# A two-layer decoder step in three-product fp32r: the product with the weight's lower half moves to the end of each unit, three bits of work move on VectorE

## Chip, core, metric

One NeuronCore of a Trainium2 chip runs the whole program. TensorE (PE; PEld is its weight load), VectorE (DVE), ScalarE (ACT), GpSimd (POOL) and SyncE (SP) run side by side and meet at semaphores. The metric is device microseconds of one execution; lower is better.

## The reference

Two layers over 288 tokens (256 of a prompt, 32 of eight samples), width 1024:

```
h = RMSNorm(x); z = h @ w_in                 # u, v, B, C, xin, gate_A, gate_B
ya = (gelu(u) * spatial_mix(RMSNorm(gelu(v)))) @ w_a
yb = (B * conv3(C * xin)) @ w_b
x += (sigmoid(gate_A) * ya + sigmoid(gate_B) * yb) @ w_o
x += PEER(RMSNorm(x))                        # 16384 experts, 8 heads, top 16 of 128 x 128 keys
x += sigmoid(RMSNorm(x) @ w_pg) * (p @ w_ple)
y = RMSNorm(x) after layer 2
```

The output also holds the convolution's last rows and the samples' normalised v.

## The kernel before

**Units.** All weights stream through SBUF in tiles of 128 x 1024, four tiles to a quad, 91 quads to a layer. A tile is a *unit*: ACT rounds the raw tile to `w_hi` (fp32r, semaphore `hi`), DVE or POOL makes the rest `w_lo = raw - w_hi` (semaphore `lo`), and PE adds up in one PSUM bank, over eight chunks c of 128 rows, three products: w_hi with the activation's upper half (line 1417), w_hi with its lower half (line 1418), w_lo with the upper half (line 1419). That is 24 matmuls. Before its first matmul a unit waits for `lo` (and for `evac`, that its bank is empty). `raw` has four slots and `w_hi`, `w_lo` two each, so ACT rounds unit j+2 once PE is done with unit j (`mm`), and DVE makes its `w_lo` behind that (`ahead`, line 865).

**Stages of a layer.** Quads 0 to 13 are w_in, 14 to 23 w_a, w_b, w_o, w_q, all with 288 columns. Then come 32 quads of the experts' u table with 256 columns: 16 in *fine segments* (POOL makes `w_lo` in halves, line 388; `lo_half` and `lo` tell PE; `mm_half` tells ACT that the first four chunks are done), 16 in *mixing quads*, where PE puts groups of small fp16 one-hot matmuls (lines 1597, 1598) between the units. Then 32 quads of the v table (lines 1621 to 1623), w_ple with PE transposes between its units, and w_pg (the gate).

**Seams.** Where one stage's output is the next one's input, the activation must be split too: ACT rounds chunk c (`upper`, semaphore `op_hi`), DVE makes the lower half (`lower` or `lower_scaled`, lines 898, 904, 1012; semaphore `op_lo`). The next stage's first unit (`first_quad`) waits for `op_lo` chunk by chunk. In the loops that end a stage, DVE does for each chunk: empty the PSUM bank, `ahead`, then `lower`.

**Squares.** Before a norm ACT squares x (`sq`, the tile `ext`), POOL adds up the eight chunks (`sum_chunks`, line 312), and PE sums over partitions with a matrix of ones (`sum_squares`, lines 1402 and 1406) behind unit 1 of the next quad (unit 2 at a layer's start). For the gate POOL adds chunks 0 to 5 and PE takes the last two itself (`direct=2`). The root (ACT) and its reciprocal (DVE, line 887) follow.

Each engine works its queue in the order of the code; there is no planner.

Of the kernel before, what the change touches and what calls it, by code (L numbers as in the profile page):

```python
# [4 lines left out]
P = 128  # L5
DEPTH = 2
D = 1024
C = D // P
# [68 lines left out]
def hybrid_trunk(nc, stream, u_rows, x_in, pe_in, conv_in, gains_in, ws_in, ws_blk_in, bias_in, keys_in,  # L77
                 y_out, conv_out, v_out):
    ctx = ExitStack()
    with ctx:  # L80
# [217 lines left out]
        def _(pool):  # L298
# [20 lines left out]
            for L in range(DEPTH):  # L319
# [113 lines left out]
                sum_chunks(L * SQUARES + 3 * C, direct=2)  # L433
# [7 lines left out]
        def _(act):  # L441
# [19 lines left out]
            for L in range(DEPTH):  # L461
# [84 lines left out]
                with act.Fori(0, 2) as i:  # L546
                    for j in range(4):
                        step(i + 2, j)
                        gelu(i * 4 + (8 + j))
                        act.wait_ge(t_ok, L * T_OPS + i * 4 + (j + 1))  # L550
                        upper(unit_ap(b_hi, i * 4 + j), unit_ap(t_op, i * 4 + j))
                        act.activation(unit_ap(sq, i * 4 + j), unit_ap(z, i * 4 + j), ACT.Square).then_inc(sq_ok, 1)
# [276 lines left out]
        def _(dve):  # L829
# [29 lines left out]
            for L in range(DEPTH):  # L859
# [71 lines left out]
                with dve.Fori(0, 2) as i:  # L931
                    for j in range(4):
                        evacuate(i + 2, j, unit_ap(z, i * 4 + (8 + j)), root[:, :])
                        normalised(0, i * 4 + j, x)
                        ahead(i + 2, j)
                        lower(i * 4 + (C + j), i * 4 + j, b_hi, b_lo, t_op)
# [70 lines left out]
                with dve.Fori(0, 2) as i:  # L1007
                    for j in range(4):
                        evacuate(i + Q_A, j, unit_ap(z, i * 4 + (40 + j)), unit_ap(z, i * 4 + (40 + j)))
                        ahead(i + Q_A, j)  # L1010
                        dve.wait_ge(op_hi, L * PREPS + i * 4 + (3 * C + j + 1))
                        dve.tensor_tensor(unit_ap(b_lo, i * 4 + j), unit_ap(z, i * 4 + (32 + j)),
                                          unit_ap(b_hi, i * 4 + j).bitcast(F32), ALU.subtract).then_inc(op_lo, 1)
# [3 lines left out]
                with dve.Fori(0, 2) as i:  # L1017
                    for j in range(4):
                        evacuate(i + Q_B, j, unit_ap(t_op, i * 4 + j), unit_ap(z, i * 4 + (48 + j)))
                        dve.wait_ge(evac, L * EVACS + i * 4 + (4 * Q_B + j + 5))  # L1020
                        dve.tensor_tensor(unit_ap(t_op, i * 4 + j), unit_ap(t_op, i * 4 + j),
                                          unit_ap(z, i * 4 + (40 + j)), ALU.add).then_inc(t_ok, 1)
                        ahead(i + Q_B, j)
                        lower(i * 4 + (4 * C + j), i * 4 + j, h_hi, h_lo, t_op)
# [307 lines left out]

# [62 lines left out]
        def _(pe):  # L1395
# [13 lines left out]
            for L in range(DEPTH):  # L1409
# [3 lines left out]
                def product(out, j, col, rhs_hi, rhs_lo, first, last):  # L1413

                    wh = w_hi[:, j % 2, col:col + P]
                    wl = w_lo[:, j % 2, col:col + P]
                    pe.matmul(out, wh, rhs_hi, start=first, stop=False)  # L1417
                    pe.matmul(out, wh, rhs_lo, start=False, stop=False)  # L1418
                    return pe.matmul(out, wl, rhs_hi, start=False, stop=last)  # L1419

                def unit(q, j, evac_q, a_hi, a_lo):

                    pe.wait_ge(lo, u0 + q * 4 + (j + 1))
                    pe.wait_ge(evac, e0 + evac_q * 4 + (j + 1))
                    for c in range(C):
                        m = product(ps[:, j, 0:T], j, c * P, a_hi[:, c, :], a_lo[:, c, :], c == 0, c == C - 1)
                    m.then_inc(mm, 1)
# [10 lines left out]

                def first_quad(q, n, skipped=0, a_hi=h_hi, a_lo=h_lo, squares=None,
                               order=range(C), until=(0, 0, 0, 0), squares_at=1, direct=0, after=0):  # L1440

                    for j in range(after, 4):
# [7 lines left out]
                        for k, c in enumerate(order):  # L1450
                            if j == 0:
                                operand(n + k + 1)
# [315 lines left out]
```

## Time and profile before

| | |
|---|---|
| time, median of 3 runs (lowest, highest) | 2280.68 us (2279.29, 2281.01) |
| span of the profiled execution | 2278.8 us |
| PE busy | 2246.9 us (99%), 15796 matmuls |
| PEld, DVE, ACT, POOL busy | 92%, 75%, 60%, 38% |
| HBM | 203 GB/s over the span |

The profiled execution was not timed by itself. Its span, from first to last instruction, is 0.5 us under the fastest run and 1.9 us under the median. Matmuls are pipelined: one of 256 columns is shown as 0.28 us long but the next starts 0.12 us later. So a wait on PE is read from the distance of two starts; "idle" in the trace counts less of it.

### The profile page before, as it was taken

To read this page: it belongs to the slowest core of one execution; us is meant where nothing else is said; L and a number is where in the kernel's file an instruction comes from. 1 tells how busy PE (TensorE), PEld (TensorE's weight loads), DVE (VectorE), ACT (ScalarE), POOL (GpSimd) and SP (SyncE) were. 2 spreads that over 40 slices of the span, in tenths; PEclk is the share of its full clock that TensorE was granted. 3 is DMA by queue.
4 is the path that set the end of the run, shared out by engine and by line. 5 is a ranking of instruction groups with operands and counts; after the bars stand their busy time and mean duration, and the time that the engine had idled before them with its cause. 6 is when DMAs were issued, how large, how long until landed. Compare 5 with 4: busy or idle time off the path is not lost.

```text
span 2278.8 us, 49787 instructions
## 1 busy us (share of the span) xinstructions
PE 2246.9 (99%) x15796; PEld 2093.8 (92%) x15796; DVE 1704.8 (75%) x3271; ACT 1369.4 (60%) x2705; POOL 865.6 (38%) x776
## 2 busy tenths in 40 slices
PE   8999999999999999999999999999999999999998
PEld 8999999999999888888899999999999998888887
DVE  6556769966888788788774567699478888887886
ACT  6544456667777555555754545566677775555555
POOL 3100108987777112111131001199877761111110
PEclk9999999999999999999999999999999999999999
DMA  6444454555444789788554445455554448888873
GB/s 220 158 142 166 162 176 166 185 184 176 156 157 157 265 300 320 265 297 283 167 183 158 139 166 181 142 187 184 179 172 157 155 163 287 298 313 268 294 269 130
DMA packets 127142, 462.94 MB, mean 203 GB/s; under 512 B 14704, under 2 KB 14864, under 8 KB 126288
## 3 DMA queue, kind: packets, MB, share of 16 engines
q1 hardware_dynamic: 106416, 385.20, 48.4%
q0 software_dynamic: 20640, 76.68, 12.0%
q8 instruction: 44, 0.72, 0.1%
q14 instruction: 42, 0.34, 0.1%
HBM read 457.87 MB, written 3.95 MB: 203 GB/s over the span
## 4 chain that ended last, share of the span: by engine, by line
PE 72%; POOL 13%; issue 9%; DVE 3%; ACT 2%; POOLq 1%; DVEq 0%; ACTq 0%
PE ps L1417 14%; PE ps L1419 13%; PE ps L1418 13%; POOL w_lo L388 12%; PE ps L1621 10%; PE ps L1623 10%; PE ps L1622 9%; PE ps L1597 1%; PE ps L1598 1%; DVE w_lo L865 1%; ACT w_hi L468 1%; POOLq L314 1%; DVE b_lo L898 0%; PE ps L1508 0%; DVE x L1344 0%
## 5 line engine op out<-in xcount | busy, mean ns | idle before, releaser
L1417 PE MATMUL ps<-h_hi,w_hi 128*128 128x256 f32 (+1 forms) x2592 | 748.5, 289 | 13.7 <-DVE h_lo L846 7.8
L388 POOL TENSOR_TENSOR w_lo<-raw,w_hi 128x512 fp32r<-128x512 f32 x508 | 648.8, 1290 | 261.1 <-ACT w_hi L490 144.3
L1418 PE MATMUL ps<-h_lo,w_hi 128*128 128x256 f32 (+1 forms) x2592 | 739.0, 285 | 0.0
L1419 PE MATMUL ps<-h_hi,w_lo 128*128 128x256 f32 (+1 forms) x2592 | 735.1, 284 | 0.0
L1417 PEld LDWEIGHTS ps<-h_hi,w_hi 128*128 128x128 f32 x2592 | 490.9, 189 | 16.7 <-issue 7.8
L1418 PEld LDWEIGHTS ps<-h_lo,w_hi 128*128 128x128 f32 x2592 | 489.9, 189 | 0.2
L1419 PEld LDWEIGHTS ps<-h_hi,w_lo 128*128 128x128 f32 x2592 | 488.1, 188 | 0.0
L468 ACT ACTIVATE w_hi<-raw 128x1024 fp32r<-128x1024 f32 x334 | 351.7, 1053 | 194.6 <-PE ps L1419 194.2
L1229 DVE TENSOR_TENSOR w_lo<-raw,w_hi 128x512 fp32r<-128x512 f32 x504 | 347.9, 691 | 128.9 <-ACT w_hi L715 87.8
L865 DVE TENSOR_TENSOR w_lo<-raw,w_hi 128x1024 fp32r<-128x1024 f32 x208 | 256.7, 1234 | 197.7 <-ACT w_hi L468 196.2
L1621 PE MATMUL ps<-w_hi,h_hi 128*128 128x512 f32 x1016 | 401.4, 395 | 0.0
L1623 PE MATMUL ps<-w_hi,h_lo 128*128 128x512 f32 x1016 | 400.0, 394 | 0.0
L1622 PE MATMUL ps<-w_lo,h_hi 128*128 128x512 f32 x1016 | 398.2, 392 | 0.0
L1417 PE MATMUL ps<-b_hi,w_hi 128*128 128x288 f32 x1152 | 345.5, 300 | 4.3 <-DVE w_lo L865 2.2
L1419 PE MATMUL ps<-b_hi,w_lo 128*128 128x288 f32 x1152 | 341.4, 296 | 0.0
L1418 PE MATMUL ps<-b_lo,w_hi 128*128 128x288 f32 x1152 | 336.2, 292 | 0.0
L715 ACT ACTIVATE w_hi<-raw 128x512 fp32r<-128x512 f32 x248 | 156.9, 633 | 200.4 <-PE ps L1623 196.0
L1623 PEld LDWEIGHTS ps<-w_hi,h_lo 128*128 128x128 f32 x1016 | 191.2, 188 | 45.4
L1622 PEld LDWEIGHTS ps<-w_lo,h_hi 128*128 128x128 f32 x1016 | 191.4, 188 | 44.0
L1621 PEld LDWEIGHTS ps<-w_hi,h_hi 128*128 128x128 f32 x1016 | 190.7, 188 | 42.5
L1417 PEld LDWEIGHTS ps<-b_hi,w_hi 128*128 128x128 f32 x1152 | 216.4, 188 | 8.8 <-DVE w_lo L865 2.4
L1418 PEld LDWEIGHTS ps<-b_lo,w_hi 128*128 128x128 f32 x1152 | 219.3, 190 | 0.3
(223 smaller groups left out, 3012.4 us busy)
## 6 DMA issues: line engine op xcount, KB each, us to landing
raw<-stream SPq DMA_DIRECT2D x730, 512.0 KB, 3.3
bias<-bias_in POOLq DMA_DIRECT2D x2, 1152.0 KB, 6.9
x_keep<-x POOLq DMA_DIRECT2D x2, 1152.0 KB, 6.4
x<-x_keep POOLq DMA_DIRECT2D x2, 1152.0 KB, 9.1
x<-x_in SPq DMA_DIRECT2D x4, 288.0 KB, 6.4
y_out<-t_op SPq DMA_DIRECT2D x4, 288.0 KB, 2.1
ws<-ws_in POOLq DMA_DIRECT2D x2, 512.0 KB, 4.0
ring<-u_rows,rows POOLq DMA_INDIRECT x44, 5.7
```

The source lines that it names most:

```text
L314: pool.drain()
L388: return pool.tensor_tensor(w_lo[:, k % 2, lo_col:hi_col], raw[:, k, lo_col:hi_col], w_hi[:, k % 2, lo_col:hi_col].bitcast(F32), ALU.subtract)
L468: act.activation(w_hi[:, j % 2, :], raw[:, j, :], ACT.Copy).then_inc(hi, 1)
L715: act.activation(w_hi[:, k % 2, 0:D // 2], raw[:, k, 0:D // 2], ACT.Copy).then_inc(v_hi, 1)
L865: dve.tensor_tensor(w_lo[:, j % 2, :], raw[:, j, :], w_hi[:, j % 2, :].bitcast(F32), ALU.subtract).then_inc(lo, 1)
L1229: dve.tensor_tensor(w_lo[:, k % 2, at:at + D // 2], raw[:, k, at:at + D // 2], w_hi[:, k % 2, at:at + D // 2].bitcast(F32), ALU.subtract). ...
L1417: pe.matmul(out, wh, rhs_hi, start=first, stop=False)
L1418: pe.matmul(out, wh, rhs_lo, start=False, stop=False)
L1419: return pe.matmul(out, wl, rhs_hi, start=False, stop=last)
L1621: pe.matmul(out, m_up, wh, start=first, stop=False)
L1622: pe.matmul(out, m_up, wl, start=False, stop=False)
L1623: m = pe.matmul(out, m_low, wh, start=False, stop=last)
```

## The change

1. **Order of products.** A unit waits for `hi` only, makes the 16 products with `w_hi` for all eight chunks, then waits for `lo` and makes the eight products with `w_lo`. In the fine segments `mm_half` now comes behind the fourth of these eight (the 20th matmul; it was the 12th). In a stage's first unit (`first_unit`) six chunks are done so, and the last two one after the other as they come; in the very first unit of the program all but the first come one by one, as before. The one-hot groups of the mixing quads keep their place in the stream.
2. **Four seams.** At the ends of quads 3, 15, 17 and 19, DVE makes the last chunk's lower half of the activation ahead of `w_lo` of the unit after next; before, behind it. At the first of them ACT also rounds the last chunk ahead of its GELU. The loops around these are written out.
3. **Gate's squares.** DVE adds chunks 0 to 6 (six adds, a drain between two) in place of POOL's chunks 0 to 5, and PE takes one chunk itself.

```diff
-                def product(out, j, col, rhs_hi, rhs_lo, first, last):
+                def with_upper(out, j, col, rhs_hi, rhs_lo, first):
                     wh = w_hi[:, j % 2, col:col + P]
-                    wl = w_lo[:, j % 2, col:col + P]
                     pe.matmul(out, wh, rhs_hi, start=first, stop=False)
                     pe.matmul(out, wh, rhs_lo, start=False, stop=False)
-                    return pe.matmul(out, wl, rhs_hi, start=False, stop=last)
+                def with_lower(out, j, col, rhs_hi, last):
+                    return pe.matmul(out, w_lo[:, j % 2, col:col + P], rhs_hi, start=False, stop=last)
+                def all_chunks(out, q, j, a_hi, a_lo):
+                    for c in range(C):
+                        with_upper(out, j, c * P, a_hi[:, c, :], a_lo[:, c, :], c == 0)
+                    pe.wait_ge(lo, u0 + q * 4 + (j + 1))
+                    for c in range(C):
+                        m = with_lower(out, j, c * P, a_hi[:, c, :], c == C - 1)
+                    m.then_inc(mm, 1)
                 def unit(q, j, evac_q, a_hi, a_lo):
-                    pe.wait_ge(lo, u0 + q * 4 + (j + 1))
+                    pe.wait_ge(hi, u0 + q * 4 + (j + 1))
                     pe.wait_ge(evac, e0 + evac_q * 4 + (j + 1))
...
+                def first_unit(q, n, a_hi, a_lo):
+                    out = ps[:, 0, 0:T]
+                    deferred = C - 2 if q else 1
+                    for c in range(deferred):
+                        operand(n + c + 1)
+                        with_upper(out, 0, c * P, a_hi[:, c, :], a_lo[:, c, :], c == 0)
+                    pe.wait_ge(lo, u0 + (q * 4 + 1))
+                    for c in range(deferred):
+                        with_lower(out, 0, c * P, a_hi[:, c, :], False)
+                    for c in range(deferred, C):
+                        operand(n + c + 1)
+                        with_upper(out, 0, c * P, a_hi[:, c, :], a_lo[:, c, :], False)
+                        m = with_lower(out, 0, c * P, a_hi[:, c, :], c == C - 1)
...
                 for c in range(C):
                     dve.wait_ge(mm, u0 + (4 * Q_O + c + 1))
                     dve.tensor_tensor(x[:, c, :], x[:, c, :], ps[:, c % 4, 0:T], ALU.add).then_inc(evac, 1)
-                    ahead(Q_O + c // 4, c % 4)
+                    if c < C - 1:
+                        ahead(Q_O + c // 4, c % 4)
                     lower_scaled(5 * C + c, c, 2, b_hi, b_lo)
+                ahead(Q_O + 1, 3)
...
+                for k in range(1, C - 1):
+                    dve.wait_ge(sq_ok, L * SQUARES + (3 * C + k + 1))
+                    a = dve.tensor_tensor(sq[:, 0, :], sq[:, 0, :], sq[:, k, :], ALU.add)
+                    if k < C - 2:
+                        dve.drain()
+                a.then_inc(sum_ok, 1)
```

How it moves instructions, at three places. First PE, within a unit of a fine segment (before), at its fourth and fifth chunk:

```order
L1417 MATMUL ps<-h_hi,w_hi 128x256
L1418 MATMUL ps<-h_lo,w_hi 128x256
L1419 MATMUL ps<-h_hi,w_lo 128x256
L1417 MATMUL ps<-h_hi,w_hi 128x256 [waits lo]
L1418 MATMUL ps<-h_lo,w_hi 128x256
L1419 MATMUL ps<-h_hi,w_lo 128x256
```

The same unit now, from its last chunk with `w_hi` to its end (lines 1426, 1427 and 1431 are the old 1417, 1418 and 1419):

```order
L1426 MATMUL ps<-h_hi,w_hi 128x256
L1427 MATMUL ps<-h_lo,w_hi 128x256
L1595 REGISTER_ALU
L1431 MATMUL ps<-h_hi,w_lo 128x256 [waits lo_half]
L1431 MATMUL ps<-h_hi,w_lo 128x256 x3
L1431 MATMUL ps<-h_hi,w_lo 128x256 [waits lo]
L1431 MATMUL ps<-h_hi,w_lo 128x256 x3
```

Both waits for `w_lo` now stand behind 16 and 20 matmuls of the unit; they stood before the first and the 13th. Second DVE, the last chunk of quad 3 (before), where t_op is the chunk, b_lo its lower half:

```order
L892 SCALAR_TENSOR_TENSOR t_op<-x,gains,root 128x288
L864 REGISTER_ALU
L865 TENSOR_TENSOR w_lo<-raw,w_hi 128x1024 [waits hi]
L897 REGISTER_ALU
L898 ISA [waits op_hi]
L898 TENSOR_TENSOR b_lo<-t_op,b_hi 128x288
```

and the same place now (each line number is one higher):

```order
L912 TENSOR_TENSOR z<-ps,root 128x288 [waits mm]
L893 SCALAR_TENSOR_TENSOR t_op<-x,gains,root 128x288
L899 TENSOR_TENSOR b_lo<-t_op,b_hi 128x288 [waits op_hi]
L866 TENSOR_TENSOR w_lo<-raw,w_hi 128x1024 [waits hi] x3
L888 RECIPROCAL root<-root 128x288 [waits rt_ok]
```

One `w_lo` has moved behind the chunk's lower half. Third DVE, at the gate, between the last half of a `w_lo` and the reciprocal of the root, before:

```order
L1317 TENSOR_TENSOR w_lo<-raw,w_hi 128x512 [waits part_hi]
L1320 TENSOR_TENSOR w_lo<-raw,w_hi 128x512 [waits hi]
L865 TENSOR_TENSOR w_lo<-raw,w_hi 128x1024 [waits hi] x2
L887 RECIPROCAL root<-root 128x288 [waits rt_ok]
L1336 TENSOR_TENSOR ps<-ps,root 128x288 [waits mm] x2
```

and now:

```order
L1322 TENSOR_TENSOR w_lo<-raw,w_hi 128x512 [waits part_hi]
L1325 TENSOR_TENSOR w_lo<-raw,w_hi 128x512 [waits hi]
L1339 TENSOR_TENSOR ext<-ext 128x288 [waits sq_ok] x6
L866 TENSOR_TENSOR w_lo<-raw,w_hi 128x1024 [waits hi] x2
L888 RECIPROCAL root<-root 128x288 [waits rt_ok]
```

Six adds stand in DVE's queue ahead of two `w_lo` and of the reciprocal; five have left POOL's.

## Rows read from the trace of the kernel before

**Rows 1.** The page: busy time of the engines (us, share of the span, instructions).

```profile
PE 2246.9 (99%) x15796; PEld 2093.8 (92%) x15796; DVE 1704.8 (75%) x3271; ACT 1369.4 (60%) x2705; POOL 865.6 (38%) x776
```

**Rows 2.** PE's waits over the whole span: waiter, releaser, us, times, longest.

```profile
PE ps L1417 <- DVE w_lo L865: 5.2, 10, 1.2
PE ps L1402 <- POOL ext L312: 3.4, 3, 1.4
PE ps L1417 <- POOL w_lo L388: 2.5, 4, 0.8
...
PE ps L1417 <- DVE b_lo L904: 1.0, 2, 0.5
PE ps L1417 <- DVE b_lo L898: 1.0, 2, 0.5
```

**Rows 3.** PE's timeline at the end of quad 3: start, us, instruction, [idle before].

```profile
66.18 0.29 PE L1419 MATMUL ps<-b_hi,w_lo 128*128 128x288 f32 x1
66.98 0.40 PE L1417 MATMUL ps<-b_hi,w_hi 128*128 128x288 f32 x1 [0.51 <-DVE b_lo L898]
67.21 0.29 PE L1418 MATMUL ps<-b_lo,w_hi 128*128 128x288 f32 x1
```

**Rows 4.** Windows in two stages: us, busy (count) by engine PE, PEld, DVE, ACT, POOL, clock.

```profile
345.00:490.00 145.00, 145.00 (x1233) 145.00 (x1233) 131.06 (x518) 93.54 (x203) 133.18 (x103) 1.00 0.55 181
...
170.00:225.00 55.00, 55.00 (x417) 55.00 (x416) 35.79 (x59) 25.02 (x38) 0.00 (x0) 1.00 0.50 168
```

**Rows 5.** PE's timeline in a fine segment: a unit's middle, then its end.

```profile
493.23 0.27 PE L1419 MATMUL ps<-h_hi,w_lo 128*128 128x256 f32 x1
493.35 0.28 PE L1417 MATMUL ps<-h_hi,w_hi 128*128 128x256 f32 x1
...
494.65 0.27 PE L1419 MATMUL ps<-h_hi,w_lo 128*128 128x256 f32 x1
495.70 0.38 PE L1417 MATMUL ps<-h_hi,w_hi 128*128 128x256 f32 x1 [0.78 <-POOL w_lo L388]
```

**Rows 6.** ACT's timeline at that unit's end.

```profile
494.20 0.61 ACT L493 ACTIVATE w_hi<-raw 128x512 fp32r<-128x512 f32 x1
```

**Rows 7.** DVE's and ACT's timelines at the end of quad 3.

```profile
65.97 0.95 DVE L898 TENSOR_TENSOR b_lo<-t_op,b_hi  x1
65.03 0.43 ACT L511 ACTIVATE b_hi<-t_op  x1
```

**Rows 8.** PE's timeline at the gate of the first layer.

```profile
1114.69 0.75 PE L1402 MATMUL ps<-ext,ones 128*128 128x288 f32 x2 [1.39 <-POOL ext L312]
1115.28 1.13 PE L1406 MATMUL ps<-ext,ones 128*128 128x288 f32 x4
```

**Rows 9.** POOL's, ACT's and DVE's timelines at that gate.

```profile
1109.58 5.05 POOL L312 TENSOR_TENSOR ext<-ext 128x288 f32<-128x288 f32 x5 [38.76 <-ACT ext L447]
1108.71 2.78 ACT L447 ACTIVATE ext<-x 128x288 f32<-128x288 f32 x8
1112.47 1.61 DVE L865 TENSOR_TENSOR w_lo<-raw,w_hi 128x1024 fp32r<-128x1024 f32 x1 [3.36 <-ACT w_hi L468]
```

**Rows 10.** DVE's timeline: two operations of which the second needs the first.

```profile
492.82 0.27 DVE L1130 RECIPROCAL ps<-total 128x18 f32<-128x18 f32 x1
493.16 0.45 DVE L1132 TENSOR_TENSOR route<-route,ps 128x288 f32<-128x288 f32 x1
```

**Rows 11.** DVE's timeline from that gate to the next layer's first units.

```profile
1116.98 1.95 DVE L887 RECIPROCAL root<-root 128x288 f32<-128x288 f32 x1 [1.27 <-ACT root L507]
1120.72 1.23 DVE L865 TENSOR_TENSOR w_lo<-raw,w_hi 128x1024 fp32r<-128x1024 f32 x1 [0.88 <-ACT w_hi L468]
1122.43 0.47 DVE L1340 TENSOR_TENSOR ps<-ps,z 128x288 f32<-128x288 f32 x1 [0.48 <-ACT ps L794]
1140.35 2.33 DVE L904 SCALAR_TENSOR_TENSOR h_lo<-x,gains,h_hi 128x288 fp32r<-128x288 f32 x3
```

**Rows 12.** PE's waits from 1100 to 1160 us.

```profile
PE ps L1417 <- DVE w_lo L865: 3.5, 4, 1.2
```

More of the change, by code:

```diff
@@ L545, in _ @@
                 act.drain()
[L546 to L552, printed above, removed]
+                for c in range(C):
+                    step(2 + c // 4, c % 4)
+                    if c < C - 1:
+                        gelu(8 + c)
+                    act.wait_ge(t_ok, L * T_OPS + c + 1)
+                    upper(b_hi[:, c, :], t_op[:, c, :])
+                    if c == C - 1:
+                        gelu(8 + c)
+                    act.activation(sq[:, c, :], z[:, c, :], ACT.Square).then_inc(sq_ok, 1)
                 step(4, 0)
@@ L930, in _ @@
                     first_v(n)
[L931 to L936, printed above, removed]
+                for c in range(C):
+                    evacuate(2 + c // 4, c % 4, z[:, 8 + c, :], root[:, :])
+                    normalised(0, c, x)
+                    if c < C - 1:
+                        ahead(2 + c // 4, c % 4)
+                    lower(C + c, c, b_hi, b_lo, t_op)
+                ahead(3, 3)
                 ahead(4, 0)
@@ L1005, in _ @@
                 dve.sem_inc(passed, 1)
[L1007 to L1013, printed above, removed]
+                for c in range(C):
+                    evacuate(Q_A + c // 4, c % 4, z[:, 40 + c, :], z[:, 40 + c, :])
+                    if c < C - 1:
+                        ahead(Q_A + c // 4, c % 4)
+                    dve.wait_ge(op_hi, L * PREPS + (3 * C + c + 1))
+                    dve.tensor_tensor(b_lo[:, c, :], z[:, 32 + c, :], b_hi[:, c, :].bitcast(F32),
+                                      ALU.subtract).then_inc(op_lo, 1)
+                ahead(Q_A + 1, 3)
                 dve.wait_ge(out_v, L * 16 + 16)
                 dve.sem_inc(passed, 1)
[L1017 to L1024, printed above, removed]
+                for c in range(C):
+                    evacuate(Q_B + c // 4, c % 4, t_op[:, c, :], z[:, 48 + c, :])
+                    dve.wait_ge(evac, L * EVACS + (4 * Q_B + c + 5))
+                    dve.tensor_tensor(t_op[:, c, :], t_op[:, c, :], z[:, 40 + c, :], ALU.add).then_inc(t_ok, 1)
+                    if c < C - 1:
+                        ahead(Q_B + c // 4, c % 4)
+                    lower(4 * C + c, c, h_hi, h_lo, t_op)
+                ahead(Q_B + 1, 3)
                 for c in range(C):
@@ L1637, in ple_unit @@
                 def ple_unit(j):
+                    pe.wait_ge(hi, u0 + (4 * Q_PLE + j + 1))
+                    for k in range(2):
+                        for c in range(CP):
+                            with_upper(ps[:, PLE_BANK[j] + k, 0:T], j, (k * CP + c) * P,
+                                       h_hi[:, 4 + c, :], h_lo[:, 4 + c, :], c == 0)
                     pe.wait_ge(lo, u0 + (4 * Q_PLE + j + 1))
@@ L1678, in _ @@
                         pe.wait_ge(x_up, L * X_UPS + (2 * C + 4))
-                    for c in range(C):
-                        m = product(ps[:, GATE_BANK[4 + j], 0:T], j, c * P, b_hi[:, c, :], b_lo[:, c, :], c == 0, c == C - 1)
-                    m.then_inc(mm, 1)
+                    all_chunks(ps[:, GATE_BANK[4 + j], 0:T], Q_PG + 1, j, b_hi, b_lo)
             for c in range(C):
```

99 lines of the change are left out of this document (53 added, 46 removed).

## The prediction

> **What bounds the kernel now.** I read the page first. PE is busy 99% of the span and no other engine comes near [rows 1]. Busy is not yet fast, so the windows come next: in the fine segments PE issues 1233 matmuls in 145 us, 117.6 ns each, in the 288-column stages 417 in 55 us, 131.9 ns each, with no idle time and the clock at its full level in both [rows 4]. That is 0.46 ns a column either way: inside the stages the kernel runs at PE's own pitch, and ACT and POOL follow PE. Nothing in the change takes products away there. What it can win is in the few places where PE stands still, so the list of PE's waits is the view that decides [rows 2]. The reader is to see four kinds: for w_lo (DVE 5.2 us in 10 waits, POOL 2.5 us in 4), for the last activation chunk at two seams (b_lo, 1.0 and 1.0 us), and for the sum of squares (3.4 us in 3).
>
> A wait costs more than its idle time. At the end of quad 3 two starts that lie 0.26 us apart at pitch lie 1.03 us apart (66.18 to 67.21), so the wait of 0.51 us cost 0.77: 0.26 us go with draining and refilling the pipeline [rows 3]. I add 0.26 us to every wait that goes.
>
> **The change, part by part.**
>
> *Products with w_lo last.* A unit may start when w_hi stands; w_lo is wanted 16 matmuls later, 2.1 us at 288 columns and 1.9 us at 256 [rows 4]. The longest wait for w_lo is 1.2 us [rows 2], so each should go, unless w_hi is late itself. Of DVE's ten, one (0.2 us, the third unit of the program) lies just ahead of the first sum of squares, where PE waits 0.6 us more for POOL: what is won there is waited for there. It counts nothing. Nine of DVE with 5.0 us, four of POOL with 2.5 us, and 13 refills of 0.26 us make 10.9 us. In two of POOL's, w_hi is late too: at 494.65 PE would go on at 494.77, and ACT's second half of w_hi ends at 494.81 [rows 5, 6]. There I leave a short wait and its refill, 0.35 us, in each layer. **10.2 us.**
>
> Against this stand two costs. First, waits are added: each unit now waits once more in its middle. A fine unit has such a wait today, at its 13th matmul, and the two starts around it are 0.12 us apart, the pitch [rows 5]. So a wait that is met costs nothing; the other end is the 0.10 us by which the second matmul behind an unmet wait comes late (0.23 for 0.13 us) [rows 3]. I take zero, since the row is for the same kind of wait. Second, mm_half comes eight matmuls (0.9 us) later, and it starts ACT's half of w_hi and then POOL's two halves of w_lo. POOL is busy 92% there, 1.29 us a half [rows 4]. From the 20th matmul of unit j ACT takes 0.6 us [rows 6] and POOL 2.6 us; the result is wanted at the 20th matmul of unit j+2, 48 matmuls or 5.6 us later. Two units of PE's own work hide it, with 2.4 us to spare. Without that cover each 0.1 us would come back in 128 units, 13 us. SP's refill of the raw slot is released later by the same 0.9 us and is wanted two units after that.
>
> The order itself could alter the pitch: no row shows eight products with w_lo in succession. The two stages differ by 0.3% a column [rows 4]; on 11,232 such matmuls, about 1,400 us, that is 4 us either way. I take zero and keep both ends.
>
> *Four seams.* Two of them show in the list, 2.0 us in four waits [rows 2], with refills 3.0 us. Will the chunk be in time? At the end of quad 3 ACT's b_hi ends at 65.46, and DVE then makes w_lo first and ends the lower half at 66.92 [rows 7]. Without w_lo ahead of it, it ends at 65.9 with 0.45 us [rows 10], at 66.4 with the 0.95 us of the row, and PE wants it at 66.31 [rows 3]; ACT rounds this chunk ahead of its GELU now, which brings about 0.3 us more. So the wait goes. The other two seams have no line in the list; a wait too short for it still costs about a refill, so I take 0.3 us in each of four places, with 0 and 0.77 as ends. **4.2 us.** What is late next is the w_lo that was moved, by about 1 us; it belongs to the unit behind, is wanted 16 matmuls into it, and is hidden by the first part alone.
>
> *The gate's squares.* POOL's adds run from 1109.58 to 1114.63, and PE stands 1.39 us [rows 8, 9]. DVE is idle for 3.36 us up to 1112.47, from 1109.11 on [rows 9]. The squares come 0.34 us apart from 1108.71, the second at about 1109.5. Of two operations on DVE of which the second needs the first, the second starts 0.07 us behind the end [rows 10]: with 0.45 us an add, six take 3.2 us and end at 1112.7. PE gets there at 1114.69 less 1.39 and a drain of 0.16, at 1113.1, or 0.3 us sooner as its unit starts sooner. The wait is gone or nearly: 2.8 us of idle time in the two gates ([rows 2], less the 0.6 us of the first sum) and 0.5 us of refills. One direct matmul less saves two passes of 0.24 us in each [rows 8], 1.0 us. **4.3 us.** The two w_lo behind the adds start 0.3 us later, and PE wants them 16 matmuls into units 2 and 3.
>
> The Trainium skill, "Vector Engine: DVE Perf Modes", section "The DRAIN you can't avoid", speaks against this part: behind every operation stands a drain of about its duration less 266 ns. By that an add would take 0.45 + 0.18 us, the six 3.8 us, and PE would wait some 0.5 us in each gate, so that the sum would come out 1 us higher. The row has 0.07 us in place of 0.18, so I don't follow it.
>
> *Between the layers* these gains can't all be kept. From the reciprocal at 1116.98 to the last h_lo at 1142.68 DVE waits only 0.88 + 0.48 us in 25.7 us [rows 11]: it is the bound there, and PE waits for it four times, 3.5 us [rows 12]. I counted 3.5 + 4 x 0.26 for these and 2.1 for the gate, 6.7 us. Sure is what DVE's own queue gives: the reciprocal starts about 0.9 us earlier (a table load on ACT holds it, though the sum comes 2 us earlier), and both waits should go, as PE delivers sooner: 2.3 us. The rest is waits for w_lo that PE now meets in mid-unit; some come back as waits for h_lo. Between 2.3 and 6.7 I take 4.5, the middle. **Less 2.2 us.**
>
> **Sum.** 10.2 + 4.2 + 4.3 - 2.2 = 16.5 us. The span of 2278.8 us becomes 2262.3; with the 1.9 us by which the median lies above the span, 2264.2 us, 0.7% faster.
>
> **Rivals.**
>
> *The waits move on.* Between the layers only DVE's queue counts (2.3 for 4.5 us), and half of the other waits for w_lo come back as waits for w_hi, since ACT rounds only 1.2 us ahead of DVE: nine waits are left there, 5.5 us with refills, half is 2.7. Time 2269. For it: two places where w_hi is late [rows 6]. Against: ACT is busy 65% in the fine segments [rows 4].
>
> *The adds on DVE come late.* DVE's b_lo took 0.95 us at a place where POOL adds too, for 0.45 alone [rows 7, 10]. Six such adds take 6.1 us and end at 1115.6, 1 us behind POOL. Each gate loses 1.0 and its gain of 1.65: 2269.5. Against: POOL's adds have left that place.
>
> *The pitch suffers.* Worse by 0.8 to 1.4%, the order eats most or all of the gain: 2276 to 2284. No row speaks for it, and none shows the order.
>
> *The added wait breaks the stream (slower).* If PE can't load weights ahead over it, each of 472 units pays 0.10 us [rows 3]: 47 us less 16.5, 2311. It decides from 0.035 us a unit. Against: the fine unit's middle [rows 5]. The Trainium skill, "TensorE: Matmul & The Clock Gate", section "Step-by-step: what each phase is for", says that PE pulls weight loads ahead of running matmuls; it doesn't say what a met wait does to that.
>
> **Numbers.** Forecast 0.66; waits move on 0.14; late adds 0.06; pitch 0.09 (same 0.06, slower 0.03); broken stream 0.03; other 0.02. This kernel's measurement can tell about 0.2% (4.6 us) from no change. Faster 0.87, same 0.07, slower 0.06. The forecast's own bounds are 4 us of pitch, 2.2 us between the layers and 1.5 us at the short seams: 2259 to 2269. With the waits that move on and the late adds the range is 2258 to 2271.
>
> **What would show it.** In the trace after: no wait for w_lo among PE's waits in the 288-column stages; no b_lo or h_lo at the ends of quads 3, 15, 17 and 19; six adds on DVE at the gate within 3.5 us, and PE at the sum without 1.4 us of idle; between the layers waits for h_lo or w_hi of about 2 us; 117.6 and 131.9 ns a matmul unchanged in the same stages. The prediction is wrong if these pitches move by more than 0.3%, or if a new releaser, ACT's w_hi above all, stands in PE's list.

## The result, and the profile after

The changed kernel takes **2257.69 us** (median of 4 runs, 2257.63 to 2257.72) against 2280.76 us of the kernel before in the same comparison (2279.29 to 2281.01): a ratio of 0.990, 95% interval 0.9887 to 0.9913. It is 1.0% faster, 23.1 us, where I had forecast 16.5 us and a range that ended at 2258.0. The sign came as forecast, and so did the waits; a part of the gain has another cause, which the prediction had put at nothing, and the time lies just outside the range, on the fast side. The profiled execution's span is 2255.9 us, 22.9 us less than before.

PE's waits over the whole span, after (waiter, releaser, us in total, times, longest), which answer to [rows 2]:

```profile
PE ps L1426 <- DVE h_lo L847: 8.2, 1, 8.2
PE ps L1426 <- DVE h_lo L905: 2.0, 3, 1.0
PE ps L1664 <- DVE m_first L1219: 1.5, 2, 0.7
```

The reader is to see what is missing: no w_lo, neither DVE's nor POOL's, no b_lo, no sum of squares. What is left are the first load (8.2 us; 7.8 before), m_first at the change to the expert units, and 2.0 us for h_lo between the layers, the amount that the prediction named.

The end of quad 3, PE's and DVE's timelines after (start, us, instruction, [idle before]); they answer to [rows 3, 7]:

```profile
65.46 0.29 PE L1426 MATMUL ps<-b_hi,w_hi 128*128 128x288 f32 x1
65.59 0.29 PE L1427 MATMUL ps<-b_lo,w_hi 128*128 128x288 f32 x1
```

```profile
64.30 0.46 DVE L899 TENSOR_TENSOR b_lo<-t_op,b_hi 128x288 fp32r<-128x288 f32 x1 [0.53 <-ACT b_hi L510]
64.67 1.22 DVE L866 TENSOR_TENSOR w_lo<-raw,w_hi 128x1024 fp32r<-128x1024 f32 x1
```

The last chunk's half ends at 64.76, 0.7 us ahead of the products that want it at 65.46, and w_lo is made behind it. The two starts are 0.13 us apart: no wait, no refill.

The gate of the first layer, DVE's and PE's timelines after, for [rows 8, 9]:

```profile
1101.95 3.14 DVE L1339 TENSOR_TENSOR ext<-ext 128x288 f32<-128x288 f32 x6 [0.40 <-ACT ext L446]
1105.00 1.22 DVE L866 TENSOR_TENSOR w_lo<-raw,w_hi 128x1024 fp32r<-128x1024 f32 x1
```

```profile
1104.24 1.23 PE L1431 MATMUL ps<-b_hi,w_lo 128*128 128x288 f32 x8
1105.30 0.65 PE L1412 MATMUL ps<-ext,ones 128*128 128x288 f32 x2
```

The six adds take 3.14 us, forecast 3.2, and end at 1105.09; PE comes at 1105.30 and stands not at all. The adds take 0.46 us each and start 0.53 us apart. That answers the one place where the Trainium skill, "VectorE: DVE Perf Modes", section "The DRAIN you can't avoid", spoke against the change: by an estimate from its drain the six would have taken 3.8 us and PE would have waited. The section excepts operations that are not held, so it doesn't say for certain that these six pay the drain; the trace shows that they don't.

Between the layers, PE's three waits after, for [rows 12]:

```profile
1127.29 0.40 PE L1426 MATMUL ps<-h_hi,w_hi 128*128 128x288 f32 x1 [0.72 <-DVE h_lo L905]
1131.56 0.37 PE L1426 MATMUL ps<-h_hi,w_hi 128*128 128x288 f32 x1 [0.97 <-DVE h_lo L905]
1132.77 0.40 PE L1426 MATMUL ps<-h_hi,w_hi 128*128 128x288 f32 x1 [0.34 <-DVE h_lo L905]
```

Now the view in which most of the missing 6 us lie. Windows of the kernel after (us, busy and count by engine PE, PEld, DVE, ACT, POOL, then clock, DMA share, GB/s), the first and last of which answer to [rows 4]:

```profile
345.00:490.00 145.00, 145.00 (x1240) 145.00 (x1239) 129.48 (x499) 89.72 (x205) 129.46 (x103) 1.00 0.58 187
350.00:480.00 130.00, 130.00 (x1111) 130.00 (x1110) 120.47 (x475) 79.72 (x186) 117.86 (x93) 1.00 0.57 186
1465.00:1595.00 130.00, 130.00 (x1111) 130.00 (x1110) 120.04 (x482) 79.31 (x185) 117.73 (x93) 1.00 0.58 186
540.00:680.00 140.00, 140.00 (x1347) 138.17 (x1346) 119.39 (x169) 104.85 (x253) 106.47 (x85) 1.00 0.48 157
170.00:225.00 55.00, 55.00 (x417) 55.00 (x416) 35.32 (x59) 25.31 (x38) 0.00 (x0) 1.00 0.52 169
```

And of the kernel before, in the fine segments of both layers and in the mixing units, which the prediction had not read:

```profile
350.00:480.00 130.00, 130.00 (x1106) 130.00 (x1105) 121.24 (x485) 83.94 (x183) 119.51 (x93) 1.00 0.56 188
1480.00:1610.00 130.00, 130.00 (x1096) 130.00 (x1095) 121.00 (x485) 83.42 (x182) 117.94 (x92) 1.00 0.56 186
540.00:680.00 140.00, 140.00 (x1339) 137.94 (x1338) 118.74 (x168) 103.91 (x251) 105.75 (x84) 1.00 0.47 157
```

PE is busy all the time in every one of these windows and its clock is full, yet the counts differ. In 130 us the old order issues 1106 products in the first layer and 1096 in the second, the new one 1111 in both. In the mixing units it is 1339 against 1347 in 140 us. A window also counts the products that reach over its ends, about two more than start in it; so the pace is better read from starts. From the first product of one fine unit to that of the next, the trace has 2.827 us for the first of these, 2.853 for the second, 2.813 after (117.8, 118.9 and 117.2 ns a product); mixing units took 3.353 us before and 3.333 after.

In the 288-column window the counts are equal, 417 and 417, but the starts are not. PE's timeline at the beginnings of successive units in that window, first with the operand b, then with h, before:

```profile
171.59 0.29 PE L1417 MATMUL ps<-b_hi,w_hi 128*128 128x288 f32 x1
...
174.76 0.29 PE L1417 MATMUL ps<-b_hi,w_hi 128*128 128x288 f32 x1
...
206.51 0.30 PE L1417 MATMUL ps<-h_hi,w_hi 128*128 128x288 f32 x1
...
209.71 0.30 PE L1417 MATMUL ps<-h_hi,w_hi 128*128 128x288 f32 x1
```

and after:

```profile
169.10 0.29 PE L1426 MATMUL ps<-b_hi,w_hi 128*128 128x288 f32 x1
...
172.28 0.29 PE L1426 MATMUL ps<-b_hi,w_hi 128*128 128x288 f32 x1
...
204.06 0.29 PE L1426 MATMUL ps<-h_hi,w_hi 128*128 128x288 f32 x1
...
207.26 0.29 PE L1426 MATMUL ps<-h_hi,w_hi 128*128 128x288 f32 x1
```

A unit with b goes from 3.173 to 3.180 us, 0.2% slower; one with h takes 3.200 in both. So the kernel before had two paces at 288 columns as well, 0.8% apart, and the new order costs a little there.

With the starts of the same unit laid side by side in the two traces, the gain divides so (us; each is the difference of the two starts behind a place less that ahead of it):

| place | forecast | measured |
|---|---|---|
| waits for w_lo outside the layer seam | 5.7 | 5.3 |
| four seams, two layers | 4.2 | 4.4 |
| gate of the first layer, and between the layers | 4.5 | 4.1 |
| gate of the second layer | 2.15 | 2.3 |
| pitch of the 256-column products | 0 (4 either way) | 5.7 |
| first sum of squares | 0 | 0.9 |
| pitch of the 288-column products | 0 | -0.8 |

The lines come to 21.9 of 22.9 us; the rest is in places of 0.1 to 0.2 us that the table leaves out. The line of the first sum is probably not the change's. In the execution profiled before, ACT waited 1.71 us at 8.56 for the load of x, in the one after it didn't, and POOL's first adds moved with it; in the profiles below, most of them of kernels with the new order, the wait at this sum lies anywhere between 0 and 1.6 us. What sets it was not tested.

### The profile page after: what moved, and what is told of

The parts are those of the page before. It is cut to its first block, busy times and chain, and to the rows that moved or that the text cites. A ratio compares the mean times of both kernels' runs of the same rounds, so it can differ in the third digit from the quotient of the medians.

```text
span 2255.9 us, 49461 instructions
## 1 busy us (share of the span) xinstructions
PE 2235.0 (99%) x15792; PEld 2088.6 (93%) x15792; DVE 1709.5 (76%) x3283; ACT 1355.8 (60%) x2705; POOL 855.5 (38%) x766
## 4 chain that ended last, share of the span: by engine, by line
PE 97%; DVE 2%; ACT 0%; DMA 0%; issue 0%; DVEq 0%; SPq 0%; ACTq 0%
PE ps L1426 21%; PE ps L1431 20%; PE ps L1427 20%; PE ps L1664 11%; PE ps L1666 11%; PE ps L1665 10%; PE ps L1620 1%; PE ps L1621 1%; PE ps L1579 1%; PE ps L1542 0%; DVE w_lo L866 0%; DVE h_lo L905 0%; PE ps L1544 0%; PE ps L1525 0%; DVE x L1354 0%; DMA raw<-stream 0%
## 5 line engine op out<-in xcount | busy, mean ns | idle before, releaser
L1426 PE MATMUL ps<-h_hi,w_hi 128*128 128x256 f32 (+1 forms) x2592 | 651.7, 290 | 10.4 <-DVE h_lo L847 8.2
L1427 PE MATMUL ps<-h_lo,w_hi 128*128 128x256 f32 (+1 forms) x2592 | 638.9, 282 | 0.0
L1431 PE MATMUL ps<-h_hi,w_lo 128*128 128x256 f32 (+1 forms) x2592 | 372.3, 284 | 0.0
L1431 PEld LDWEIGHTS ps<-h_hi,w_lo 128*128 128x128 f32 x2592 | 338.3, 189 | 0.1
L1426 PE MATMUL ps<-b_hi,w_hi 128*128 128x288 f32 x1152 | 313.2, 299 | 0.0
L1427 PE MATMUL ps<-b_lo,w_hi 128*128 128x288 f32 x1152 | 310.1, 295 | 0.0
L716 ACT ACTIVATE w_hi<-raw 128x512 fp32r<-128x512 f32 x248 | 156.9, 633 | 200.8 <-PE ps L1666 193.5
L719 ACT ACTIVATE w_hi<-raw 128x512 fp32r<-128x512 f32 x248 | 157.1, 633 | 96.9 <-PE ps L1666 96.7
```

The source lines that it names most:

```text
L716: act.activation(w_hi[:, k % 2, 0:D // 2], raw[:, k, 0:D // 2], ACT.Copy).then_inc(v_hi, 1)
L719: act.activation(w_hi[:, k % 2, D // 2:D], raw[:, k, D // 2:D], ACT.Copy).then_inc(hi, 1)
L1431: return pe.matmul(out, w_lo[:, j % 2, col:col + P], rhs_hi, start=False, stop=last)
```

## The experiments

The theory after the result: the order of the products itself makes the 256-column products faster, with no wait in it, and all else is as forecast. The rival: what looks like pitch are waits too short for the list, or comes from the other two parts.

**The first part alone.** The edit: PE's order and waits as in the change, the rest as before, with two chunks of the gate's squares left to PE (`direct=2`). Against the kernel before, cut to the wait of a unit:

```diff
-                    pe.wait_ge(lo, u0 + q * 4 + (j + 1))
+                    pe.wait_ge(hi, u0 + q * 4 + (j + 1))
...
```

> The kernel before with the first part alone: products with w_lo last, the four seams and the gate's adds as before. Theory A (the order itself makes the 256-column matmuls faster, by 13 ns a unit in the first layer's fine segment, 40 ns in the second's, 20 ns in the mixing units, as the two traces differ): 5.3 us of pitch, 5.3 us of waits for w_lo outside the layer seam, about 1.7 us in the layer seam: 12.3 us, 2268.5 us. Theory B (the pitch came from elsewhere, from the seams' or the gate's code): 7 us, 2273.8 us, and fine units of 2.827 and 2.853 us as before. Either way PE's list shows b_lo at the seams and POOL's sum at the gate again.

Measured: 2267.19 us (before 2279.0; ratio 0.9947, interval 0.9931 to 0.9964). Fine units 2.813 us in both layers, mixing units 3.333. The window of the first layer's fine segment, and PE's waits:

```profile
350.00:480.00 130.00, 130.00 (x1111) 130.00 (x1111) 121.07 (x482) 79.31 (x184) 117.75 (x93) 1.00 0.58 186
```

```profile
PE ps L1402 <- POOL ext L312: 4.2, 3, 1.7
...
PE ps L1416 <- DVE b_lo L898: 1.0, 2, 0.5
PE ps L1416 <- DVE b_lo L904: 1.0, 2, 0.5
```

The pitch came with the order alone, and the waits of the two other parts stand as before, POOL's longer (1.7 us for 1.4) since PE arrives sooner. Theory A.

**The wait for w_lo back at the start of the unit.** The order stays new.

```diff
-                    pe.wait_ge(hi, u0 + q * 4 + (j + 1))
+                    pe.wait_ge(lo, u0 + q * 4 + (j + 1))
...
```

> The changed kernel with PE waiting for w_lo at the start of each unit as before, the order of the products unchanged. Theory A (order makes the pitch): the waits for w_lo come back, 5.3 us outside the layer seam and 2 us in it, the fine units stay at 2.813 us: 2265 us. Theory B (the fine units were longer because the start of each waited a few ns for w_lo, too short for the list): the fine units go back to 2.827 and 2.853 us too: 2270 us or more.

Measured: 2269.13 us; fine units 2.813 us. PE's waits:

```profile
PE ps L1426 <- DVE w_lo L866: 5.9, 11, 1.2
PE ps L1426 <- POOL w_lo L388: 2.9, 4, 0.8
```

As to the pitch this is theory A: the waits are back and the pitch stays. The time is 4 us above what I gave for it, since I had counted the waits as the difference of the two traces, and here they are more: among others, the seams now make w_lo last, so that PE waits for it where it didn't before (0.58 us at 283.39).

**The second and third part alone**, on the kernel before: the hunks on ACT, DVE and POOL, and `direct=1`.

> The kernel before with the second and third parts alone: four seams and the gate's adds on VectorE, products in the old order. From the differences between the two traces, 4.4 us at the seams and 4.7 us in the gates: 9.1 us less up to 1 us in the layer seam, 2271.7 to 2272.7 us. If the parts only work together (b_lo comes in time, but w_lo, made last, is then waited for at the next unit's start, 1 us later than before), the seams bring nothing: 2276 us.

Measured: 2273.76 us (ratio 0.9977, interval 0.9967 to 0.9986), 5.2 us instead of the 8 to 9 expected. One row of PE's timeline, at the end of quad 19:

```profile
282.43 0.40 PE L1427 MATMUL ps<-b_hi,w_hi 128*128 128x288 f32 x1 [0.59 <-DVE w_lo L866]
```

There the wait for b_lo (0.51 us) became one for w_lo (0.59 us) at the next unit's start. The seam at quad 3 kept 0.6 us in each layer, the others little. Besides, the fine segments of this execution stood at 2.853 us in both layers. So three of the four seams need the first part. The whole change wins 9.5 us over the first part alone (11.3 if each is taken from the kernel before in its own comparison, 2280.76 and 2279.0 us), and these two parts without it 5.2.

**The old order in part of the 256-column units.** I meant to put it back into the fine segments and the mixing units; the kernel as run has it in the mixing units and in `ple_unit`, and its fine segments are as in the change.

```diff
-                            with_upper(out, j, c * P, h_hi[:, c, 0:SEQ], h_lo[:, c, 0:SEQ], c == 0)
...
+                            m = product(ps[:, j, 0:SEQ], j, c * P, h_hi[:, c, 0:SEQ], h_lo[:, c, 0:SEQ],
+                                        c == 0, c == C - 1)
```

> The changed kernel with the old order of products, and the old waits, in the fine segments and the mixing units alone. Theory A: pitch 5.3 us and POOL's four waits 2.9 us come back: 2265.9 us, fine units 2.827 or 2.853 us, which of the two depends on where the segment starts. Theory B: the waits alone, 2260.6 us.

Measured: 2261.56 us. The mixing units go back to 3.353 us, by the window of the first layer's:

```profile
540.00:680.00 140.00, 140.00 (x1337) 138.00 (x1335) 118.49 (x168) 104.64 (x252) 105.46 (x84) 1.00 0.48 155
```

The two mixing stretches take 2.05 us more each, 1.3 of pitch and a wait for POOL; together about the 3.9 us by which the span grew. It shows the order's price in the mixing units, says nothing of the fine segments, and its expectation can't be read against it.

**The kernel before, once more, unchanged.**

> The kernel before once more, unchanged. Theory A1 (in the old order a fine unit settles into one of several repeating patterns, 2.813, 2.827 or 2.853 us a unit, and which one is decided anew at each stall ahead of it): the four fine stretches (two in each layer, parted by the wait for POOL's w_lo) stand at other values than 2.827, 2.853, 2.853, 2.827, and the span moves by up to 4 us with them. Theory A2 (the pattern belongs to the place in the program): the same four values.

Measured: 2279.49 us, one run. Its fine segments, first layer and second:

```profile
350.00:480.00 130.00, 130.00 (x1095) 130.00 (x1095) 121.08 (x487) 83.36 (x181) 117.93 (x92) 1.00 0.54 185
1480.00:1610.00 130.00, 130.00 (x1106) 130.00 (x1105) 121.09 (x484) 84.00 (x183) 119.34 (x93) 1.00 0.54 186
```

The two have changed places: 2.853 us in the first layer, 2.827 in the second, with the same code. Within each layer the one turns into the other at the stall for POOL's w_lo near the end or at the six transposes that stand two units behind it, here and in the first execution. This is theory A1: the old order has two repeating patterns, and where the stream is broken it can fall into the other. Which break decides isn't shown: in the run of the second and third part alone, and in the next one, the units stay at 2.853 us behind both. The two patterns may account for a part of the spread of the kernel before, whose runs go from 2277.66 to 2282.05 us over these comparisons; they can't be all of it, for kernels with the new order spread too (2268.54 to 2269.91 us with the wait at the start, 2261.80 to 2263.31 below without the seams), while the changed one's four lie within 0.1 us.

**The old order in the fine segments alone**, one of the two places that I had meant above.

```diff
-                                with_upper(out, j, c * P, h_hi[:, c, 0:SEQ], h_lo[:, c, 0:SEQ], c == 0)
...
+                                m = product(ps[:, j, 0:SEQ], j, c * P, h_hi[:, c, 0:SEQ], h_lo[:, c, 0:SEQ],
+                                            c == 0, c == C - 1)
```

> The changed kernel with the old order of products, and the old waits, in the fine segments alone (128 units; the mixing units keep the new order). Theory A (the old order settles at 2.827 or 2.853 us a unit, the new one at 2.813): 0.9 to 2.6 us a layer of pitch, and 0.65 us a layer as the wait for POOL's w_lo comes back: 2260.8 to 2264.1 us, with 2262.4 for one stretch pair at each value. Theory B (the old order can settle at 2.813 too, behind other stalls): 2259.0 us.

Measured: 2264.52 us, 2.853 us a unit in both layers:

```profile
350.00:480.00 130.00, 130.00 (x1096) 130.00 (x1095) 120.53 (x474) 83.70 (x183) 117.57 (x92) 1.00 0.57 185
1475.00:1605.00 130.00, 130.00 (x1096) 130.00 (x1095) 118.57 (x473) 83.82 (x183) 117.64 (x92) 1.00 0.57 185
```

Theory A, with both layers at the slower value and 0.4 us above its range: the fine stretches grow by 3.07 and 3.14 us with their waits, which is most of the 6.8 us.

**Seams and gate taken out one by one.** First the seams, on ACT as well as on DVE, cut to DVE's part at quad 3:

```diff
-                    lower(C + c, c, b_hi, b_lo, t_op)
-                ahead(3, 3)
+                        ahead(i + 2, j)
+                        lower(i * 4 + (C + j), i * 4 + j, b_hi, b_lo, t_op)
```

> The changed kernel with VectorE making w_lo ahead of the last activation chunk's half at the four seams, as before. If the seam's parts pay by themselves: waits for b_lo of 0.5 us at quads 3 and 17 to 19 come back, 4.4 us, 2262.1 us. If products-last alone had hidden them: 2257.7 us.

Then the gate's adds, with `direct=2` on PE:

```diff
-                for k in range(1, C - 1):
-                    dve.wait_ge(sq_ok, L * SQUARES + (3 * C + k + 1))
...
+                sum_chunks(L * SQUARES + 3 * C, direct=2)
```

> The changed kernel with the gate's squares summed by GpSimd, and two direct matmuls at the sum, as before. The two gates lose what they won by the milestones, 2.3 us each, and as PE now comes 0.3 us sooner, its wait is 1.7 us instead of 1.4; VectorE's reciprocal comes later, of which the layer seam, bound by VectorE, gives nothing back: 2262.2 to 2262.8 us. If the layer seam hides the first gate's part: 2260 us.

Measured: 2262.33 us without the seams and 2262.70 us with the gate on POOL, 4.6 and 5.0 us above the change. PE's waits of the second:

```profile
PE ps L1408 <- POOL ext L312: 4.4, 3, 1.7
```

Both parts pay in full once the first is there, and the layer seam hides nothing of the gate.

**Other orders, to find what sets the pitch.** Four kernels, each run once, have another order in three of each four units; each unit's time is that from its first product to the next unit's.

```diff
+                            if j == 1:
+                                pairs = [(wh[c], r[c]) for r in (hh, hl) for c in range(C)]
+                            elif j == 2:
+                                pairs = [(wh[c], r[c]) for c in (0, 2, 4, 6, 1, 3, 5, 7) for r in (hh, hl)]
...
```

> The changed kernel with another order of the 16 products with w_hi in three of each four fine units: all h_hi, then all h_lo (second unit); even chunks first (third); the two swapped in every odd chunk (fourth). If the order of weights and operands sets the pitch, a unit of one kind stands apart from 2.813 us by 10 ns or more, up or down, at every position alike; if only the spacing behind the last stall does, all four are 2.813 us.

Measured, first to fourth unit: 2.813, 2.840, 2.829, 2.825 us; 2259.46 us in all. Order does set the pitch, and none of these beats the new one.

```diff
+                        elif j == 2:
+                            seq = [(t, k) for k in (0, 1, 2) for t in range(TILES)]
...
```

> The changed kernel with another order of the twelve 512-column products in three of each four expert units: with w_lo last for each bank (second unit), first products of both banks, then second, then third (third), the same with w_lo last (fourth). Pitch now 231 ns. If products that follow each other into the same bank hold each other up, the third and fourth are faster by several ns a product; if only the columns count, all are 231 ns within 1 ns.

Measured: the even expert units take 2.757 us and the odd ones 2.796, in the changed kernel and here alike, whatever the order; 2257.34 us. Neither the bank nor the order counts at 512 columns. Why odd units are slower stays open.

```diff
+                            if j == 1:
+                                seq = up[0] + [p for c in range(C) for p in (up[2][c], up[1][c])]
+                            elif j == 2:
+                                seq = [p for c in range(C) for p in (up[1][c], up[0][c])] + up[2]
+                            elif j == 3:
+                                seq = [p for c in range(C) for p in (up[0][c], up[2][c], up[1][c])]
```

> The changed kernel with other orders in three of each four fine units: all products of w_hi with h_hi, then w_lo and w_hi alternating (second unit, no two in a row with the same weights); pairs with h_lo first (third, two in a row with the same weights); the triples w_hi, w_lo, w_hi (fourth, no two in a row with the same weights). Theory W (a product goes out sooner now and then only where it has the weights of the one ahead; without such pairs each takes 118.3 ns as the eight with w_lo do): 2.840, 2.813 and 2.840 us for these three. Theory N (the pattern hangs on the whole sequence behind the last stall, not on the weights): the second and fourth stand between 2.813 and 2.853 us with no such split.

Measured: 2.813, 2.813, 2.849 us for the second to fourth, 2.825 for the first; 2259.67 us in all. The second unit never has the same weights twice in a row and is as fast as the new order: theory W falls. What the fast stretches have in common is that the moving operand goes back and forth between h_hi and h_lo (116.7 ns a product); where it walks along h_hi from one chunk to the next, as in the eight products with w_lo, each takes 118.3 ns. From this came the next one.

```diff
+                            lows = {1: (0, 4, 1, 5, 2, 6, 3, 7), 2: (0, 2, 1, 3, 4, 6, 5, 7)}.get(j, range(C))
...
```

> The changed kernel with other orders in three of each four fine units: the eight products with w_lo in the chunk order 0, 4, 1, 5, 2, 6, 3, 7 (second unit) and 0, 2, 1, 3, 4, 6, 5, 7 (third); the sixteen with w_hi alternating between h_hi and h_lo, but of neighbouring chunks, so that each two with the same h chunk have other weights (fourth). Theory M (products whose moving operand alternates between h_hi and h_lo take 116.7 ns, those that stay in h_hi 118.3 ns, whatever the weights): all four units 2.813 us, as the eight with w_lo stay in h_hi in any chunk order. Theory D (what counts is how far the next operand lies from the last one, in whichever array): the second or third unit is faster, to 2.800 us. Theory O (neither; the pattern hangs on the whole sequence): the fourth stands 10 ns or more above 2.813 us.

PE's timeline, rows at which units begin (third, fourth, first, second unit):

```profile
399.97 0.28 PE L1607 MATMUL ps<-h_hi,w_hi 128*128 128x256 f32 x1
...
402.77 0.28 PE L1607 MATMUL ps<-h_hi,w_hi 128*128 128x256 f32 x1
...
405.60 0.28 PE L1607 MATMUL ps<-h_hi,w_hi 128*128 128x256 f32 x1
...
408.43 0.28 PE L1607 MATMUL ps<-h_hi,w_hi 128*128 128x256 f32 x1
...
411.23 0.28 PE L1607 MATMUL ps<-h_hi,w_hi 128*128 128x256 f32 x1
```

The kernel took 2257.45 us. The units with the products of w_lo in a mixed chunk order take 2.800 us (402.77 less 399.97, 411.23 less 408.43): theory D. But the fourth took 2.824, and the first, whose order is the new one, 2.829 behind it, as theory O has it. So the step from chunk to chunk counts, as theory D has it, and what a unit inherits from the one ahead counts as well; no single rule covers all orders that were run.

**Better versions.** First, two of the waits that are left.

```diff
-                    for chunks in (range(5), range(5, C)):
+                    for chunks in (range(5), range(5, 6), range(6, 7), range(7, C)):
...
-                gate(C - 1)
-                add_gated(C - 1)
-                next_lower(C - 3)
+                next_lower(C - 3)
+                gate(C - 1)
+                add_gated(C - 1)
...
+                            pe.wait_ge(m_hi, L * KEYS + e + 1)
+                            for tile in range(TILES):
+                                up = m_first[:, 0, tile * P:tile * P + P]
```

> The changed kernel with two of its remaining waits attacked. At the layer seam VectorE makes the half of chunk 5 ahead of the last gate's product and sum, and PE takes chunks 5, 6 and 7 of the next layer's first two units one at a time for both units: of 1.31 us of idle time for h_lo and two refills of 0.26 us some 1.3 us should go. At the first expert unit PE makes the four products with the high half of m_first while VectorE still makes the low half: 0.45 of 0.75 us in each layer. Sum 2.2 us: 2255.5 us. If the halves of chunks 6 and 7 come later by as much as chunk 5's comes sooner, only the expert unit's 0.9 us are left: 2256.8 us.

Measured: 2256.44 us (2256.37 to 2256.80), 1.25 us below the change, of 2.2 expected. PE's waits:

```profile
PE ps L1426 <- DVE h_lo L905: 1.0, 2, 0.7
PE ps L1660 <- ACT m_first L701: 0.8, 2, 0.4
PE ps L1426 <- ACT w_hi L467: 0.7, 1, 0.7
```

m_first went as planned (1.5 to 0.8 us) and h_lo from 2.0 to 1.0. But a new wait stands there: the first two units now end together, their weight slots come free late, and ACT's w_hi for the unit behind is 0.7 us late.

Second, the chunk order of the products with w_lo, on top of this.

```diff
-                            for c in range(C // 2):
+                            for c in (0, 2, 1, 3):
                                 m = with_lower(out, j, c * P, h_hi[:, c, 0:SEQ], False)
...
-                            for c in range(C // 2, C):
+                            for c in (4, 6, 5, 7):
...
```

> e11_seam_and_first_expert with the eight products with w_lo in the chunk order 0, 2, 1, 3, 4, 6, 5, 7 in the fine segments and in the mixing units, 256 units. Theory D (a step to the neighbouring chunk of the same array costs 1.6 ns a product more on average): 13 ns a unit in both kinds, 2.800 us a fine unit and 3.320 us a mixing unit, 3.4 us less: 2253.0 us. If the order of the mixing units' products is set anew by each one-hot group: 1.7 us less, 2254.7 us.

> The same order of the products with w_lo in the 288-column units as well, some 200 of them. If the pitch of 288 columns follows the same rule, 13 ns a unit: 2.6 us less than e14_lower_order_fine, 2250.4 us. If it doesn't (its steps are not as regular as those of 256 columns): the same time as e14_lower_order_fine.

Measured: 2253.10 us (ratio to before 0.9879, interval 0.9862 to 0.9895) with the order in the 256-column units, where 2253.0 was expected, and 2256.70 us with it in the 288-column units too. The windows of the first kernel (a fine segment, the mixing units):

```profile
350.00:480.00 130.00, 130.00 (x1117) 130.00 (x1116) 120.55 (x474) 79.91 (x186) 118.37 (x94) 1.00 0.56 186
540.00:680.00 140.00, 140.00 (x1351) 138.20 (x1350) 119.79 (x169) 105.38 (x255) 106.99 (x85) 1.00 0.48 158
```

A fine unit takes 2.800 us from start to start, 116.7 ns a product, and a mixing unit 3.320, as theory D had it. At 288 columns the same order is worse: a unit with the operand b takes 3.200 us where it took 3.180, and one with h 3.200 to 3.254 where it took 3.200. The first of the two is the fastest kernel of this study, 4.6 us below the change.

## Why the prediction was wrong

The step that failed is the sentence "I take zero and keep both ends" for the pitch. It measured 5.7 us faster at 256 columns, against the 4 us either way that were to be its ends; 0.8 us of it was lost again at 288. By the prediction's own test, a pitch that moves by more than 0.3%, this is the failure: the fine units moved by 0.5% in the first layer and 1.4% in the second. The bound was worked out from two stages that differ by 0.3% a column [rows 4]. That difference comes from the counts: by starts the two windows give 117.8 and 132.6 ns, 0.1% apart a column. How far a stage differs from itself was not looked at. One of the windows was a fine segment, and I read only one; the second layer's stands 0.9% away from it in the same trace, with no idle time and a full clock in both. The other window holds units at 3.173 and at 3.200 us. Two windows of one stage would have shown that the old order has no single pitch, and a bound of 0.9% on 6,144 products of 256 columns at 117.6 ns would have been 6.5 us. The forecast's own bounds fit the root of the sum of squares of its three (4, 2.2 and 1.5 us give 2259); with 6.5 for 4 that is 2257, just below what was measured. It would have been a wider range, not a reason for the gain: nothing in the trace of before says which way the order moves the pitch. The rival "the pitch suffers" looked at the same unknown from the wrong side. The 0.9 us of the first sum are luck as far as is known; without them the time would have been some 2258.6 us, inside the range, and the pitch as wrong as it is.

The other steps held. *Products with w_lo last*: every wait went, for 5.3 of 5.7 us outside the layer seam; the short waits for w_hi that I left at POOL's two places are 0.11 us of idle time at one in the first layer (490.47), and below what the trace counts as idle at the other; those units are 0.27 and 0.18 us longer than their neighbours, for the 0.35 us that were left at each. The added wait in mid-unit costs nothing that can be seen, so the rival of the broken stream is out: the units with h at 288 columns take 3.200 us with it and without, those with b 0.007 us more, where the rival had 0.10. mm_half's 0.9 us found its cover: no wait for w_lo in the fine segments. *Four seams*: 4.4 for 4.2 us, and the 0.3 us put down for the short ones is what they gave (0.27 and 0.41, 0.25 and 0.42). The prediction said that the first part hides the w_lo that was moved; what that is worth, the third experiment shows: without the first part three of the four seams bring little, because w_lo is then late in place of b_lo. *The gate*: 2.3 us in the second layer for 2.15, with the adds in 3.14 us for 3.2, so late adds are out too. *Between the layers*: 4.1 for 4.5 us, with h_lo in the place of w_lo and 2.0 us of idle time, as DVE's queue bounds it.

"The waits move on" is half true in the layer seam, where it was counted, and nowhere else.

## What to carry to other kernels

Where an engine is busy all the time, read its pitch before taking it as fixed: from the start of one unit to the start of the next, in several stretches of the same code and in each repetition. Stretches of the same code that differ with no idle time mean that the pitch is not given by the columns alone, and a change of order may move it. A wait that is moved behind work that doesn't need its data can be worth more by what it lets other edits do: the seams won 4.6 us behind the first part and about 1.2 without it. Ask of each reordering which slot it frees later; the version that cut the wait for h_lo got part of it back as a wait for w_hi.

## What the runs showed of the hardware

The same instructions, in the same program, ran at two steady paces, 2.827 and 2.853 us for 24 products, and changed from one to the other only where the stream was broken; two executions of one kernel had them the other way round. With the 24 products in the new order the pace was 2.813 in every profile of a kernel whose fine units all have it. It is an order effect of 0.5 to 1.4%, regular to the nanosecond, at 256 columns; at 512 columns the order made no difference, and at 288 an order that helped at 256 cost 20 ns a unit with the operand b. At 288 columns the paces also went with the operand: 3.173 us a unit with b and 3.200 with h, in the old order. The Trainium skill, "TensorE: Matmul & The Clock Gate", section "Back-to-back issue gap", gives the columns at 2.4 GHz and 2.5 ns more for a single matmul by itself, and says that in a stream the weight loads count too; by the first, 256 columns would take an estimated 109 ns. No run here came to it (116.7 to 118.9 ns a product by the starts of units, with the granted clock at 1.00), and the measurements decide. What makes the paces is open: not the reuse of weights, and not the moving operand's distance alone. Whether it is where the operands lie in memory was not tested.
